# Modulation vectors as plain fp32 products in four column groups of the array, in place of split products

## The reference, cut to what matters

```python
for l in range(2):
    mod = silu(c) @ w_mod[l] + b_mod[l]            # [1, 2048] @ [2048, 6144]
    shift, scale, gate = split(mod, 3)
    cmod = silu(c_ctx) @ w_mod[l] + b_mod[l]
    cshift, cscale, cgate = split(cmod, 3)
    h  = rmsnorm(x,  norm_g[l]) * (1 + scale)  + shift
    hc = rmsnorm(cx, norm_g[l]) * (1 + cscale) + cshift
    ...                                            # projections of h and hc, attention, y
    x  = x  + gate  * (y  @ w_o[l])
    cx = cx + cgate * (yc @ w_o[l])                # layer 0 alone
```

## Time and profile before

| | |
|---|---|
| three runs | 2667.44, 2669.62, 2670.50 us; median 2669.62 us |
| profiled execution | 2672.01 us, of which the span of instructions is 2670.2 us |
| TensorE, products | busy 2561.0 us, 96% of the span, 12228 instructions |
| VectorE, ScalarE, GpSimd | 53%, 49%, 8% |
| mean granted TensorE clock | 0.985 of full speed |
| weights moved by SyncE's queue | 394.92 MB of 464.80 MB in all |

### The profile page before, as it was taken

One profiled execution on the slowest core, in us unless ns is written; L12 is line 12 of the kernel. 1 busy time (PEld: TensorE's weight loads), 2 busy tenths in 40 slices (PEclk: granted clock), 3 DMA queues, 4 the chain that ended last, 5 costly groups with the idle time before them and its releaser, 6 DMA issues. The chain is left out here.

```text
span 2670.2 us, 32472 instructions
## 1 busy us (share of the span) xinstructions
PE 2561.0 (96%) x12228; PEld 1999.4 (75%) x12228; DVE 1407.8 (53%) x2245; ACT 1296.1 (49%) x1967; POOL 220.6 (8%) x314
## 2 busy tenths in 40 slices
PE   5999999999999999999999999999998999999998
PEld 2567777777778766677777677977877887888776
DVE  5754444445554455465564445576555544444454
ACT  6644333334543444465455454545555545664553
POOL 1000001001000000000112100001010001111100
PEclk8999999999999999999999999999999999999999
DMA  8766534333322666557545445766564567667554
GB/s 314 250 233 232 186 97 121 107 94 110 95 80 80 221 206 206 186 188 232 166 146 178 138 146 169 211 200 188 166 189 148 185 207 214 181 182 233 166 180 132
DMA packets 230091, 464.80 MB, mean 174 GB/s; under 512 B 17346, under 2 KB 42240, under 8 KB 228656
## 3 DMA queue, kind: packets, MB, share of 16 engines
q1 hardware_dynamic: 209104, 394.92, 46.9%
q0 software_dynamic: 20832, 67.81, 8.0%
HBM read 431.89 MB, written 30.77 MB: 173 GB/s over the span
## 5 line engine op out<-in xcount | busy, mean ns | idle before, releaser
L1351 DVE TENSOR_TENSOR w_lo<-raw,w_hi 128x1024 fp32r<-128x1024 f32 (+4 forms) x762 | 897.1, 1193 | 1013.7 <-ACT w_hi L1076 1011.7
L1884 PE MATMUL pp<-w_hi,hT_hi 128*128 128x512 f32 (+3 forms) x2904 | 1175.3, 405 | 3.2 <-DVE w_lo L1351 2.2
L1886 PE MATMUL pp<-w_hi,hT_lo 128*128 128x512 f32 (+3 forms) x2904 | 1119.9, 386 | 0.0
L1885 PE MATMUL pp<-w_lo,hT_hi 128*128 128x512 f32 (+3 forms) x2904 | 1118.7, 385 | 0.0
L1076 ACT ACTIVATE w_hi<-raw 128x1024 fp32r<-128x1024 f32 (+4 forms) x762 | 772.0, 1030 | 690.0 <-PE pp L1886 662.7
L1884 PEld LDWEIGHTS pp<-w_hi,hT_hi 128*128 128x128 f32 x2904 | 550.1, 189 | 146.0 <-issue 42.0
L1886 PEld LDWEIGHTS pp<-w_hi,hT_lo 128*128 128x128 f32 x2904 | 549.1, 189 | 107.0
L1885 PEld LDWEIGHTS pp<-w_lo,hT_hi 128*128 128x128 f32 x2904 | 551.2, 190 | 96.2 <-issue 7.2
L1230 ACT ACTIVATE arena<-pY 128x512 f32<-128x512 f32 (+2 forms) x114 | 62.0, 544 | 132.7 <-PE pY L2038 101.2
L911 POOL DMA_DIRECT2D scratch_u<-ust x46 | 33.7, 733 | 924.6 <-ACT ust L1134 924.6
L1879 PE MATMUL pY<-w_hi,cT 128*4 128x512 f32 x192 | 80.4, 419 | 18.4 <-DVE w_lo L1351 18.1
(11 more groups left out here) (286 smaller groups left out, 1792.3 us busy)
## 6 DMA issues: line engine op xcount, KB each, us to landing
raw<-in_w_mod_dram SPq DMA_DIRECT2D x192, 512.0 KB, 4.9
raw<-in_w_in_dram SPq DMA_DIRECT2D x168, 512.0 KB, 3.7
raw<-in_e_w_in_dram SPq DMA_DIRECT2D x104, 512.0 KB, 3.8
raw<-in_w_o_dram SPq DMA_DIRECT2D x64, 512.0 KB, 3.9
raw<-in_o_w_in_dram SPq DMA_DIRECT2D x64, 512.0 KB, 4.1
raw<-in_w_out_dram SPq DMA_DIRECT2D x64, 512.0 KB, 3.7
raw<-in_w_in_dram SPq DMA_DIRECT2D x56, 440.0 KB, 3.5
scratch_u<-ust POOLq DMA_DIRECT2D x35, 512.0 KB, 4.0
```

The lines of the kernel that those rows point to most:

```text
L1351: dve.tensor_tensor(w_lo[:, g.n % SPLIT, 0:n], raw[:, g.n % RAW, 0:n], w_hi[:, g.n % SPLIT, 0:n].bitcast(F32), ALU.subtract).then_inc(lo_d ...
L1884: pe.matmul(dst, hT_hi[:, kk, o:o + P], hi[:, k, :], start=a, stop=False)
L1885: pe.matmul(dst, hT_hi[:, kk, o:o + P], lo[:, k, :], start=False, stop=False)
L1886: ins = pe.matmul(dst, hT_lo[:, kk, o:o + P], hi[:, k, :], start=False, stop=z)
```

## The change

Modulation groups are no longer split. TensorE reads their fp32 weights from `raw` and multiplies with the fp32 `cT` of two columns, one fp32 product for each K tile. K tile K writes rows 32*(K%4) and the next, so four K tiles in a row go to four different column groups of the array and to four places of one bank. The order is changed so that modulation groups always come in pairs, four K tiles in a row. The banks Y and X1 still alternate from chunk to chunk.

ScalarE now copies the eight result rows by four copies of two rows each into `parts`, a buffer of its own that is zero elsewhere; its row 2 is the bias. The selecting product runs over 98 rows. A gate chunk gets such a product as well (the sum is written as two rows, which ScalarE copies into `rows`), and its later spreading product reads two rows.

`raw` buffers of modulation groups come free when TensorE has used them, those of ordinary groups when VectorE has split them. Splits are counted without the modulation groups, and start no sooner than four groups ahead.

```diff
-AHEAD = SPLIT - 1
+AHEAD = 4
...
-        for g in self.groups[SPLIT:]:
-            g.split_at = self.groups[g.n - SPLIT].q1
+        self.cut = [g for g in self.groups if g.ch.kind != "mod"]
+        for n, g in enumerate(self.cut):
+            g.s = n
+            g.split_at = max(self.cut[n - SPLIT].q1 if n >= SPLIT else 0, self.groups[max(0, g.n - AHEAD)].q0)
...
-    def run(self, ch, mods=(), each=0, upto=None):
+    def run(self, ch, mods=(), every=1, upto=None):
...
-            for _ in range(each):
-                if mods:
-                    self.put(*mods.pop(0))
+            if j % every == every - 1:
+                for _ in range(2):
+                    if mods:
+                        self.put(*mods.pop(0))
...
-            self.run(Chunk(f"y0_{n}", "gate", "e_w_in", 4608 + c, 512, 4, ycol=c, ks=turned if n == 3 else None))
+            ch = Chunk(f"y0_{n}", "gate", "e_w_in", 4608 + c, 512, 4, ycol=c, ks=turned if n == 3 else None)
+            if n < 3:
+                self.run(ch)
+            else:
+                mod1 = self.run(ch, mod1)
...
-            mod1 = self.run(ch, mod1, 3 if n == 1 else 2, 5 if n == 3 else None)
+            mod1 = self.run(ch, mod1, upto=5 if n == 3 else None)
...
-            gate1 = self.run(Chunk(f"c_q{n}", "u", "o_w_in", 512 * n, 512, 2, dst="u1", layer=1), gate1, 1)
-        self.run(Chunk("c_kv", "u", "o_w_in", 1024, 512, 4, dst="u1", layer=1), gate1, 2)
+            gate1 = self.run(Chunk(f"c_q{n}", "u", "o_w_in", 512 * n, 512, 2, dst="u1", layer=1), gate1, 2)
+        self.run(Chunk("c_kv", "u", "o_w_in", 1024, 512, 4, dst="u1", layer=1), gate1)
...
                 if g.n >= RAW:
-                    sp.wait_ge(lo_done, g.n - RAW + 1)
+                    p = groups[g.n - RAW]
+                    if p.ch.kind == "mod":
+                        sp.wait_ge(quanta, p.q1)
+                    else:
+                        sp.wait_ge(lo_done, p.s + 1)
...
+                ch, n = C[name], mod_n[name]
+                if n >= 1:
+                    pool.wait_ge(filled["O"], left["O", ("cols", mods[n - 1])])
+                pool.dma_start(parts[2:3, :], D["b_mod"][ch.layer:ch.layer + 1, ch.c0:ch.c0 + 512]).then_inc(bias_here, 16)
...
-                    act.activation(rows[r:r + 4, s, :], src[0:4, :], ACT.Copy).then_inc(done, 1)
+                    for r in (0, 32, 64, 96):
+                        ins = act.activation(parts[r:r + 2, :], src[r:r + 2, :], ACT.Copy)
+                    ins.then_inc(done, 1)
...
+            def mod_quantum(g):
+
+                ch, slot = g.ch, g.n % RAW
+                pe.wait_ge(raw_here[slot], 16 * (g.n // RAW + 1))
+                if g.j == 0:
+                    begin(ch.bank[0], "acc", ch.name, 0)
+                b = bank[ch.bank[0]]
+                for k, K in enumerate(g.ks):
+                    r = 32 * (K % 4)
+                    ins = pe.matmul(b[r:r + 2, :], cT[:, K, :], raw[:, slot, 512 * k:512 * k + 512], start=K < 4, stop=K >= 12)
+                ins.then_inc(quanta, 1)
...
-                    if ch.kind == "mod":
-                        dst = bank[ch.bank[0]][0:4, 0:ch.W]
-                        pe.matmul(dst, cT[:, K, :], hi[:, k, :], start=a, stop=False)
-                        ins = pe.matmul(dst, cT[:, K, :], lo[:, k, :], start=False, stop=z)
-                        continue
...
+                p = parts[0:98, :]
+                if C[name].block is None:
+                    pe.matmul(b[0:2, :], keep[0:98, C_SEL:C_SEL + 2], p, start=True, stop=True).then_inc(filled["O"], 1)
+                    return
                 for k in range(4):
-                    ins = pe.matmul(b[:, 2 * k:2 * k + 2], rows[r:r + 5, s, 128 * k:128 * k + 128], keep[r:r + 5, C_SEL:C_SEL + 2], start=True, stop=True)
+                    ins = pe.matmul(b[:, 2 * k:2 * k + 2], p[:, 128 * k:128 * k + 128], keep[0:98, C_SEL:C_SEL + 2], start=True, stop=True)
```

More of the change, by code:

```diff
@@ L135, in __init__ @@
     def __init__(self):
-        self.groups, self.slots, self.chunks, self.C = [], [], [], {}
+        self.groups, self.slots, self.chunks, self.C, self.cut = [], [], [], {}, []
         self.layers()
@@ L376, in schedule @@
                 add(ch.q0 + 1, "bias", ch.name)
-                if ch.block is not None:
-                    add(ch.q1 + 1, "cols", ch.name)
+                add(ch.q1 + 1, "cols", ch.name)
             if ch.kind == "res":
@@ L645, in build @@
         ust = sb("ust", [P, 4, 512])
-        rows = sb("rows", [P, 2, 512])
+        rows = sb("rows", [P, 512])
+        parts = sb("parts", [P, 512])
         keep = sb("keep", [P, C_KEEP])
-        cT = sb("cT", [P, KT_, 4], F32R)
+        cT = sb("cT", [P, KT_, 2])
         mod_cols = sb("mod_cols", [P, 64, 2])
@@ L672, in build @@
         h_made = sem("h_made")
-        bias_here = [sem(f"bias_here{n}") for n in range(2)]
-        gate_bias_here = sem("gate_bias_here")
+        bias_here = sem("bias_here")
         scale_made = sem("scale_made")
@@ L889, in setup @@
                 pool.memset(half_neg, -0.5).then_inc(setup_done, 1)
-                pool.wait_ge(setup_done, 1)
+                pool.memset(parts[:, :], 0.0).then_inc(setup_done, 1)
+                pool.wait_ge(setup_done, 2)
             def bias(name):
[L894 to L904, removed]
+                ch, n = C[name], mod_n[name]
+                if n >= 1:
+                    pool.wait_ge(filled["O"], left["O", ("cols", mods[n - 1])])
+                pool.dma_start(parts[2:3, :], D["b_mod"][ch.layer:ch.layer + 1, ch.c0:ch.c0 + 512]).then_inc(bias_here, 16)
             def store(name, half):
@@ L1102, in evac @@
                 if ch.kind == "mod":
[L1103 to L1110, removed]
-                            act.wait_ge(filled["O"], left["O", ("gate", f"out0_{ch.row}")])
-                    act.activation(rows[r:r + 4, s, :], src[0:4, :], ACT.Copy).then_inc(done, 1)
+                    n = mod_n[name]
+                    if n >= 1:
+                        act.wait_ge(filled["O"], left["O", ("cols", mods[n - 1])])
+                    act.wait_ge(setup_done, 2)
+                    for r in (0, 32, 64, 96):
+                        ins = act.activation(parts[r:r + 2, :], src[r:r + 2, :], ACT.Copy)
+                    ins.then_inc(done, 1)
                     return
@@ L1139, in evac, with cols @@
                     act.activation(pair, pair, ACT.Silu).then_inc(silued, 1)
+            def cols(name):
+                ch = C[name]
+                if ch.block is not None:
+                    return
+                act.wait_ge(filled["O"], left["O", ("cols", name)])
+                if ch.layer == 1:
+                    act.wait_ge(filled["X0"], left["X0", ("gate", f"out0_{ch.row}")])
+                    act.wait_ge(filled["O"], left["O", ("gate", f"out0_{ch.row}")])
+                r = 32 * ch.row
+                act.activation(rows[r:r + 2, :], pO[0:2, :], ACT.Copy).then_inc(freed["O"], 1)
             def sq_x(t):
@@ L1332, in _ @@
             setup()
-            for g in groups[:AHEAD]:
-                split(g)
-            ahead = AHEAD
+            ahead = 0
             for q, todo in enumerate(plan.at):
@@ L1339, in _ @@
                         mine[e[0]](*e[1:])
-                while ahead < len(groups) and groups[ahead].split_at <= q:
-                    split(groups[ahead])
+                while ahead < len(W.cut) and W.cut[ahead].split_at <= q:
+                    split(W.cut[ahead])
                     ahead += 1
@@ L1801, in _ @@
                     "g_log": g_log, "g_less": g_less_, "g_finish": g_finish, "fl_add": fl_add, "fl_min": fl_min_}
-            setup()
-            for g in groups[:AHEAD]:
-                split(g)
-            ahead = AHEAD
+            ahead = 0
             for q, todo in enumerate(plan.at):
@@ L1907, in gate @@
                     c = C_SEL + 2 + 128 * v
-                    pe.matmul(b, keep[r:r + 5, c:c + 128], rows[r:r + 5, s, :], start=True, stop=True).then_inc(filled[name_], 1)
+                    pe.matmul(b, keep[r:r + 2, c:c + 128], rows[r:r + 2, :], start=True, stop=True).then_inc(filled[name_], 1)
             def x_turn(l, K, t0):
```

68 lines of the change are left out of this document (32 added, 36 removed).

## The result

Before: 2668.61 us (median of 4 runs, 2667.44 to 2670.50). After: 2723.70 us (4 runs, 2720.12 to 2729.15), ratio 1.0207, 95% interval 1.0187 to 1.0228: 55 us slower, where 34 us faster was forecast, and above the range's end of 2692. The profiled execution took 2721.64 us, with a span of 2719.8 against 2670.2.

A forecast was written before the change was run, and what follows sets the result against it. TensorE, busy 96% of the span, was taken as the bound. Terms -49 + 8 + 14 - 5 - 2 + 2 - 2 = -34 on the profiled 2672.0 us gave 2638, or 2635.6 as median; range 2603 to 2692.

The forecast's parts named there:

- The pair: 64 pairs of modulation groups outside the front: four fp32 products side by side take 1.10 us for 1.86; -49 us.
- In line: Rival, each of 96 pairs: the four products don't overlap, 3.44 us a pair; +132 us, median 2802; chance 0.14.
- two at a time: Rival, at the pairs: only two products run together, 1.72 us a pair; +6 to +14 us, 2680; chance 0.10.
- third rival: At each of 64 pairs, changing the tiling mode drains TensorE, 0.35 us each; +22 us on the forecast, 2658; chance 0.07.
- The longer copy: At 16 chunk ends outside the front, four ScalarE copies make TensorE stand still 0.9 us; +14 us (5 to 30).
- waits of before that were to go: Layer 1's scale and shift: three TensorE waits behind splits, 10 us with half clock, partly go; -5 us (-10 to +2).
- small things: Minor effects: shorter step at selecting products, -2 us; weight loads in c_q0 and c_q1 just hidden, +2 us (0 to +20).
- Half clock behind waits: Layer 1's scale and shift: products at half clock behind three existing waits, counted within the 10 us there.
- The selecting product: Gate chunks: eight new fp32 products of 512 columns, 0.95 us each, 1.0 with entry; +8 us (7 to 9).
- The front: To about 150 us: first part -11 us, then stretches of 18.3 and 20.7 us, +9; together -2 us (-20 to +15).
- The rival of held buffers: The ring of six raw buffers becomes the bound: front +15 us, c_q0 and c_q1 +18; 2668 us; chance 0.07.

The follow-up runs named there:

- run 9: The changed kernel with all K tiles in one column group (rows 0 and 1) and one copy of two rows; 2819.51 us, one run.
- run 3: The changed kernel with splits no sooner than three groups ahead (AHEAD 3 in place of 4); 2684.29 us, ratio 1.0062 to the kernel before.
- run 1: The changed kernel with selecting products of gates and layer 1 one ordinary group later, bias loads five slots later; 2668.21 us, ratio 0.9999 to before.
- run 4: The changed kernel with eight raw and three split buffers in place of six and four; 2669.63 us, ratio 1.0004 to the kernel before.
- run 5: The changed kernel with five raw buffers in place of six, four split buffers kept; 2807.39 us, ratio 1.0523 to the kernel before.

## Why the prediction was wrong, step by step

- **The pair:** right in its mechanism. 0.97 us to the next start and 1.17 with its steps, for the 1.10 taken, which for 64 whole pairs is -44 for -49. What the trace shows is -34: eight pairs are cut in two (8 us), and behind another TensorE stood 4 us for weights and their split (959.4 to 964.4). In line (3.53) and two at a time are out. The drain of the third rival was there in part: 0.2 us of steps for the 0.35 it would have asked. By the Trainium skill, TensorEngine Tiling (Array Packing), section Key Properties, a change of tiling mode drains the engine; the trace agrees that steps in and out are slower, and run 9 shows the same ones with a single column group.
- **The longer copy:** the step that failed. I wrote "It stands still 0.9 us" and kept "30 if ScalarE is also in a split of 1.05" as the far end. With the waits of before that were to go, the sum held +9 for this; measured were +38. Where nothing stands before the copy the wait is 1.16 us (run 3; 0.9 forecast), which for 16 chunks is some 19 us: the four copies were mis-sized (2.37 for 2.06). The other 25 us are that the copy started late, by 0.2 to 6.7 us, in all 16 chunks. In nine of them ScalarE stood idle before a split until its load landed, after the chunk's last product had started. In the other seven, the longest wait among them, it was busy with squares or copies of ordinary results, and in six of these with a split too. I had worked out in "small things" that an ordinary group's load goes out only two periods before its use and is "just hidden" from TensorE, and did not ask what else is queued on ScalarE behind the split that waits for it. Moving the split behind the copy (run 3, waits 24.7 us), the consumer later (run 1, 4.5) or the loads sooner (run 4, 30.3) each takes a part of the 43.3 away.
- **Half clock behind waits:** outside the front only as a part of the waits that were to go, and in no term for the new ones. The earlier trace rows showed it, and it came behind 12 of the 16 waits: +14 us.
- **The selecting product:** +12 where the sum had +6 (8 and -2), as the 98-row ones run in part at half clock (1.84 for 1.05).
- **The front:** its first part began at 54.3, for 52.5. A plain stretch is 18.1, as predicted (18.3). The stretch with turns of x was to be 20.7 and is 25.7 and 26.4: ordinary products at half clock, turns, selecting products and the load all stand in one chain, and the burst of loads lands late. With a last wait of 3.6 us before `b_q1` this made +17.5 for -2. Eight buffers bring `b_q1` 24 us sooner, so the ring was the right cause and its price was too low.
- **The rival of held buffers** had 0.07 and 2668 us. It named the right resource, with the cost in the front (+15) and by DMA rate in `c_q0` and `c_q1` (+18). In the front it was near (+17.5 in place of -2). In `c_q0` and `c_q1` the price was -2 us; it fell in the stages with `w_o` and gate 0 instead, through ScalarE's order. By run 5 a buffer less costs 84 us more, so the ring was at its edge.

Together: from the forecast's -34 to the +50 of the spans are 84 us. Waits before selecting products are 29 of them, the front 20, the pairs 15, half clock 14 and selecting products 6.

The 12 us of slower steps can be split by other products of the two traces. Before's fp32r products of four columns have 0.23 in and out. An fp32 product with 128 rows and 128 columns (L2038 in before) has 0.23 in and 0.31 out. With 64 rows (L2085 in before) it has 0.32 in and 0.34 out, as the two-column ones have. So the step out is mostly the data type, and the step in shows only where fp32 and a small operand come together.

Open: eight `raw` with four split buffers was not tried; nor was an order in which no pair is cut in two.

## What to carry to other kernels

When a buffer is released by its last reader and no longer by a copy of it, find the place in each engine's order where the next load is first waited for, and list what stands behind that place: here a 2.4 us copy behind such waits, and behind ScalarE's other work, cost more (38 us, and 14 of half clock) than the pairs had saved (34). ScalarE's average of 42% busy says nothing of an engine that stands at the head of its queue. A short chain through another engine (last product, copy, selecting product) is best given slack in the order, and one instruction in place of four, before the work around it is made faster.

## What the runs showed of the hardware that was not expected

- Four fp32 products in four column groups, all on the same 128 input rows, start 7 ns apart and take 0.97 us together, against 3.53 for the four in one group. Reading four weight tiles at once cost nothing visible: two of them alone, in a cut pair, take 0.96. The Trainium skill, TensorE: Matmul & The Clock Gate, Part 3 (Packing small matmuls), has 2.38 times for three groups; here it is 3.6 for four.
- Copies of two rows by ScalarE cost what the copy of four rows did: 2.37 us for four, 0.59 each and 0.60 from start to start, with none of the overlap that I had put in.
- TensorE's granted clock followed most of its waits, and not by their length alone. Behind 12 of the 16 waits outside the front, 4 to 12 ordinary products are 0.43 apart (1.2 in place of 2.4 GHz), behind one of 1.6 us as behind one of 6.7; behind 1.9, 2.0 and 3.1 us in gate 0 and 0.5 in gate 1 there are none. So a wait can cost more than its length: in run 1, 58 us behind the front for 39 us of waits.
